# Output projections placed earlier among the sample streams, inverse roots on VectorE, expert loads issued in pieces, and a reordered rank chain

## The reference

```python
xn = rmsnorm(x, norm_mix_g)
q, k, v, f, B, C, h = split(xn @ w_in)            # 3*512 + 8 + 3*512 columns
o_a = forgetting_attention(q, k, v, f)            # 8 heads of 64; a stream also reads 128 cached rows
o_b = B * causal_conv3(C * h)                     # 512 channels
x = x + concat(rmsnorm(o_a, g_a), rmsnorm(o_b, g_b)) @ w_out
t = rmsnorm(x, norm_ffn_g)
g = top1(softmax(t @ w_rg + b_rg))                # 4 groups
e1, e2 = top2(softmax(t @ w_re[g] + b_re[g]))     # 8 experts in each group
x = x + sum(w_e * (silu(t @ gate_e) * (t @ up_e)) @ down_e for e in (e1, e2))
y = rmsnorm(x, norm_final_g)
```

## Time and profile before

| | |
|---|---|
| median of 3 runs | 546.57 us |
| the profiled execution's own time | 542.85 us |
| its span | 540.9 us |
| TensorE busy | 463.1 us (86%) |
| TensorE weight loads | 259.7 us (48%) |
| VectorE busy | 188.1 us (35%) |
| ScalarE busy | 125.2 us (23%) |
| mean granted clock of TensorE | 0.912 |
| bytes moved by DMA | 131.34 MB |

### The profile page before, as it was taken

How to read it: one execution, slowest core, us unless ns; L and a number is a source line. 1 busy time by engine, 2 the same in 40 slices (tenths; PEclk the granted TensorE clock), 3 DMA queues, 4 the chain that set the end, 5 groups by cost and what they waited for, 6 DMA issues and landing times.

```text
span 540.9 us, 6899 instructions
## 1 busy us (share of the span) xinstructions
PE 463.1 (86%) x2687; PEld 259.7 (48%) x2687; DVE 188.1 (35%) x555; ACT 125.2 (23%) x272; POOL 17.8 (3%) x49
## 2 busy tenths in 40 slices
PE   5999999999997979998569999799897998597580
PEld 4556545555656645644567357253533434152120
DVE  2200002424534425461644751244351425123234
ACT  4123213234224516554401110010010101010014
POOL 6000020000000000000000000001000000000000
PEclk9799999999996989998669996899898999889685
DMA  8997720000004942000805999999999999999702
GB/s 283 376 387 197 244 109 19 2 0 0 1 0 161 414 184 79 21 1 1 349 1 216 423 411 417 415 416 421 412 422 412 420 413 420 417 418 417 294 1 117
DMA packets 38232, 131.34 MB, mean 243 GB/s; under 512 B 10346, under 2 KB 10390, under 8 KB 30008
## 3 DMA queue, kind: packets, MB, share of 16 engines
q1 hardware_dynamic: 36928, 127.13, 60.0%
q10 hardware_dynamic: 664, 2.14, 1.0%
q0 software_dynamic: 608, 1.62, 0.8%
HBM read 127.68 MB, written 3.19 MB: 242 GB/s over the span
## 4 chain that ended last, share of the span: by engine, by line
PE 53%; DMA 31%; SPq 6%; DVE 4%; ACT 3%; issue 2%; DVEq 0%; ACTq 0%
PE bank L1465 50%; DMA gu_ring<-in_w_expert_gate_up 26%; SPq L533 3%; DMA r_xs<-in_cache_k 3%; DMA gu_ring<-in_w_in 2%; PE bank L1679 1%; PE bank L1585 1%; ACT L766 1%; DVE X L1453 1%; ACT r_xT L971 1%; SPq L545 1%; SPq L542 1%; PE bank L1649 0%; ACT r_xT L813 0%; DVE r_qz L1168 0%
## 5 line engine op out<-in xcount | busy, mean ns | idle before, releaser
L1465 PE MATMUL bank<-gu_ring,r_xT 128*32 128x512 f32 (+1 forms) x560 | 88.6, 670 | 23.5 <-DMA gu_ring<-in_w_expert_gate_up 23.5
L1465 PE MATMUL bank<-r_xT,gu_ring 128*128 128x384 f32 x192 | 66.4, 506 | 2.3 <-DMA gu_ring<-in_w_in 2.3
L1465 PEld LDWEIGHTS bank<-gu_ring,r_xT 128*32 128x32 f32 (+1 forms) x560 | 28.8, 128 | 80.3 <-issue 80.1
L1465 PEld LDWEIGHTS bank<-r_xT,gu_ring 128*128 128x128 f32 x192 | 37.6, 198 | 28.3 <-DMA gu_ring<-in_w_in 2.5
L1465 PE MATMUL bank<-BT,r_qz 128*128 128x128 f32 x384 | 46.4, 282 | 4.2 <-DVE BT L1271 4.2
L1465 PE MATMUL bank<-r_xs 128*128 128x512 f32 x96 | 49.8, 649 | 0.0
L1465 PEld LDWEIGHTS bank<-BT,r_qz 128*128 128x128 f32 x384 | 44.9, 197 | 10.2 <-issue 10.2
L1465 PE MATMUL bank<-r_xT,dn_ring 128*128 128x384 f32 x128 | 42.6, 486 | 0.0
L1345 DVE TENSOR_TENSOR X<-X,bank 128x512 f32<-128x512 f32 x48 | 33.0, 688 | 23.3 <-PE bank L1465 22.8
L1465 PE MATMUL bank<-dn_ring,V 128*32 128x512 f32 x256 | 31.3, 633 | 7.1 <-ACT V L917 4.3
L907 ACT ACTIVATE r_kT<-bank 128x256 f32<-128x256 f32 x8 | 3.1, 384 | 142.7 <-PE bank L1465 142.7
(11 more groups left out here) (293 smaller groups left out, 493.9 us busy)
## 6 DMA issues: line engine op xcount, KB each, us to landing
gu_ring<-in_w_expert_gate_up SPq DMA_DIRECT2D x64, 1024.0 KB, 18.8
dn_ring<-in_w_expert_down SPq DMA_DIRECT2D x32, 1024.0 KB, 20.3
gu_ring<-in_w_in SPq DMA_DIRECT2D x4, 2048.0 KB, 11.9
dn_ring<-in_w_in SPq DMA_DIRECT2D x2, 2048.0 KB, 19.1
gu_ring<-in_w_out SPq DMA_DIRECT2D x2, 2048.0 KB, 9.2
r_xs<-in_cache_k SPq DMA_DIRECT2D x8, 256.0 KB, 3.6
r_xs<-in_cache_v SPq DMA_DIRECT2D x8, 256.0 KB, 6.9
X<-in_x SPq DMA_DIRECT2D x3, 512.0 KB, 4.2
```

The source lines that it names most:

```text
L1465: return te.matmul(out, lhsT, rhs, start=start, stop=stop, **kw)
```

## The change

Output projections, sums and routing of tiles 0 and 1 have new steps; the twelve input projections leave out every fourth unit; the sums of tile 2 no longer go through the jobs. All inverse roots are made by VectorE: a first value from the bits of the number and three steps. x2's transposes read X itself, and the gain of the ffn norm goes into the router's weights (whose layout changes with it) and, with the root, into the gained rows. Quad 0's weights are issued in five places. The spare expert is chosen on VectorE from the counts, and loaded before quad 1. `gate_up(0)` stands before keys and slot weights; the overflow table and `swiglu(0)` before the picks of quad 1.

```diff
@@ jobs
         for f in range(3 * CT):
-            jobs_at.setdefault(1 + f, []).append(("ChB"[f % 3], f // 3))
-        first_oB = 3 * CT + 4
-        jobs_at[first_oB - 1] = [("ssB",)]
-        for i, keys in enumerate((
-                [("ssA", 0), ("oB", 0, 0)], [("oB", 0, 1)], [("oA", 0, 0)], [("oA", 0, 1)],
-                [("ssA", 1), ("oB", 1, 0)], [("oB", 1, 1)], [("x2", 0), ("oA", 1, 0)], [("lg", 0), ("oA", 1, 1)],
-                [("oB", 2, 0)], [("oB", 2, 1)], [("x2", 1)])):
-            jobs_at[first_oB + i] = keys
-        AFTER = [("lg", 1), ("ssA", 2), ("oA", 2, 0), ("oA", 2, 1), ("x2", 2), ("lg", 2)]
+            jobs_at.setdefault(1 + f + f // 3, []).append(("ChB"[f % 3], f // 3))
+        jobs_at.update({
+            2 * H: [("ssA", 0)], 2 * H + 1: [("oA", 0, 0)], 2 * H + 2: [("ssB",), ("oA", 0, 1)], 2 * H + 3: [("oB", 0, 0)],
+            2 * H + 4: [("ssA", 1), ("oB", 0, 1)], 2 * H + 5: [("oA", 1, 0)], 2 * H + 6: [("oA", 1, 1)],
+            2 * H + 7: [("oB", 1, 0), ("x2", 0)], 2 * H + 8: [("lg", 0), ("oB", 1, 1)], 2 * H + 9: [("oB", 2, 0)],
+            2 * H + 10: [("x2", 1), ("oB", 2, 1)], 2 * H + 11: [("lg", 1)]})
+        LAST_ROWS = 2 * H + 4
+        AFTER = [("oA", 2, 0), ("oA", 2, 1), ("x2", 2), ("lg", 2)]
@@ SyncE
+            sp.wait_ge(g_full, 2 * CT + TT)
+            for half in range(2):
+                load_up(0, 2, half)
+            sp.wait_ge(g_full, g_of["C", CT - 1] + 1)
+            load_down(0, 0)
+            load_down(0, 1)
+            sp.wait_ge(g_full, g_of["h", CT - 1] + 1)
+            load_down(0, 2)
+            load_down(0, 3)
             sp.wait_ge(s_full, 2 * H)
             for b in range(2, 4):
                 sp.dma_start(ck[b], a["cache_k"][b]).then_inc(ld_ck[b], 16)
             sp.wait_ge(g_full, g_of["B", CT - 1] + 1)
             for half in range(2):
-                for h in (2, 3):
-                    load_up(0, h, half)
-            for h in range(WIDE):
-                load_down(0, h)
-            sp.wait_ge(g_full, g_of["ssB",] + 1)
-            sp.dma_start(gbc, a["norm_ffn_g"].partition_broadcast(P)).then_inc(ld_gain, 16)
+                load_up(0, 3, half)
             for b in range(4, NB):
...
+                if b == 6:
+                    sp.wait_ge(g_full, g_of["ssB",] + 1)
+                    sp.wait_ge(last_done, CT)
+                    sp.dma_start(gbc, a["norm_ffn_g"].partition_broadcast(P)).then_inc(ld_gain, 16)
...
-            sp.wait_ge(g_full, g_of["oA", TT - 1, 1] + 1)
-            for half in range(2):
-                for h in (0, 1):
+            for h, key in ((1, ("oB", TT - 1, 1)), (0, ("oA", TT - 1, 1))):
+                sp.wait_ge(g_full, g_of[key] + 1)
+                for half in range(2):
                     load_up(0, h, half)
+            load_spare()
             for n in range(1, QUADS):
...
-                if n == 1:
-                    load_spare()
@@ ScalarE, after the loop
             square_a(TT - 1)
-            estimate(("ssA", TT - 1))
-            square(TT - 1)
+            act.wait_ge(st_out, 16 * 4)
+            square_last(0)
+            square_last(1)
             x2_evac(TT - 1)
-            estimate(("nr2", TT - 1))
-            scale_rows(TT - 1)
@@ VectorE
-            def inv_sqrt(out, n0, n1, done, count, ready=None):
-
-                dve.wait_ge(done, count)
-                link(v.tensor_tensor(nt[:, n0:n1], nr0[:, n0:n1], nr0[:, n0:n1], ALU.mult))
-                link(v.tensor_tensor(nt[:, n0:n1], nt[:, n0:n1], nv[:, n0:n1], ALU.mult))
-                link(v.tensor_scalar(nt[:, n0:n1], nt[:, n0:n1], -0.5, 1.5, ALU.mult, ALU.add))
-                ins = v.tensor_tensor(out, nt[:, n0:n1], nr0[:, n0:n1], ALU.mult)
+            def inv_sqrt(out, n0, n1, ready=None):
+
+                x, z, w = nv[:, n0:n1], nr0[:, n0:n1], nt[:, n0:n1]
+                link(v.tensor_single_scalar(z.bitcast(i32), x.bitcast(i32), 1, ALU.logical_shift_right))
+                link(v.tensor_scalar(z.bitcast(i32), z.bitcast(i32), -1.0, GUESS, ALU.mult, ALU.add))
+                for three in (-3.0, -12.0, -768.0):
+                    if n1 - n0 == 1:
+                        link(v.scalar_tensor_tensor(w, z, x, z, ALU.mult, ALU.mult))
+                    else:
+                        link(v.tensor_tensor(w, z, z, ALU.mult))
+                        link(v.tensor_tensor(w, w, x, ALU.mult))
+                    link(v.scalar_tensor_tensor(z, w, three, z, ALU.add, ALU.mult))
+                ins = v.tensor_single_scalar(out, z, -1.0 / 8192.0, ALU.mult)
...
-            job_evac(("lg", 1))
-            job_evac(("ssA", TT - 1))
-            rstd(("ssA", TT - 1))
+            dve.wait_ge(*g_place[g_of["lg", 1]])
+            route(1)
+            gained_rows(1)
+            dve.wait_ge(ssz_full, 1)
+            link(v.tensor_scalar(nv[:, TT - 1:TT], bS[0][:, 0:1], 1.0 / A, EPS, ALU.mult, ALU.add))
+            inv_sqrt(rs_ab[:, TT - 1:TT], TT - 1, TT)
             job_evac(("oA", TT - 1, 0))
             job_evac(("oA", TT - 1, 1))
+            rstd2_last()
             gained_rows(TT - 1)
-            nv2(TT - 1)
-            dve.wait_ge(*g_place[g_of["lg", 1]])
-            route(1)
-            rstd2(TT - 1)
             job_evac(("lg", TT - 1))
...
             dve.wait_ge(rk_full, 1)
-            dve.wait_ge(cnt_full, 1)
-            link(v.tensor_copy(rk[:, :, :], bT[0][:, 0:TT * E].rearrange("p (t e) -> p t e", t=TT)))
+            ranks = bT[0][:, 0:TT * E].rearrange("p (t e) -> p t e", t=TT)
             for c in range(2):
-                link(v.tensor_tensor(ohr[:, :, :], oh[:, c, :, :], rk[:, :, :], ALU.mult))
-                link(v.reduce_sum(pos[:, c, :], ohr[:, :, :], AX))
+                ins = v.tensor_tensor(ohr[:, c, :, :], oh[:, c, :, :], ranks, ALU.mult)
+            link(ins)
+            link(v.reduce_sum(pos[:, :, :], ohr[:, :, :, :], AX))
...
+            pick_step(0)
+
+            dve.wait_ge(cnt_full, 1)
+            link(v.tensor_copy(cnt[:, :], bS[1][:, 0:E]))
+            link(v.tensor_scalar(e0[:, :], cnt[:, :], float(SLOTS), float(E), ALU.is_le, ALU.mult))
+            link(v.tensor_tensor(e0[:, :], e0[:, :], iota_e[:, :], ALU.add))
+            link(v.tensor_reduce(e0_key[:, 0:1], e0[:, :], AX, ALU.min))
+            v.tensor_scalar(spare_reg[:, 0:1], e0_key[0:1, 0:1], float(E - 1), None, ALU.min).then_inc(spare_set, 1)
...
+            ins.then_inc(rw_done, 1)
+            overflow_table()
+            swiglu(0)
+            dve.wait_ge(keys_full, 1)
+            pick_step(1)
...
-            v.tensor_scalar(nv[:, 0:TT], ss[:, 0:TT], 1.0 / D, EPS, ALU.mult, ALU.add).then_inc(nv3_done, 1)
+            link(v.tensor_scalar(nv[:, 0:TT], ss[:, 0:TT], 1.0 / D, EPS, ALU.mult, ALU.add))
+            inv_sqrt(rs3[:, :], 0, TT)
             for t in range(TT):
-                v.tensor_tensor(X[:, t, :], X[:, t, :], gbc, ALU.mult).then_inc(y3_done, 1)
-            dve.wait_ge(y3_done, TT)
-            inv_sqrt(rs3[:, :], 0, TT, nr3_done, 1)
-            for t in range(TT):
-                v.tensor_scalar(yo[t], X[:, t, :], rs3[:, t:t + 1], None, ALU.mult).then_inc(out_done, 1)
+                v.scalar_tensor_tensor(yo[t], X[:, t, :], rs3[:, t:t + 1], gbc, ALU.mult, ALU.mult).then_inc(out_done, 1)
@@ TensorE
-            for key in AFTER:
-                job(key)
+            job(("oA", TT - 1, 0))
+            last_squares()
+            job(("oA", TT - 1, 1))
+            job(("x2", TT - 1))
+            job(("lg", TT - 1))
...
             pick_rows(0)
+            gate_up(0)
...
             ins.then_inc(w_full, 1)
-            gate_up(0)
```

259 lines of the change are left out of this document (126 added, 133 removed).

## The result

The changed kernel takes **515.51 us** (median of 4 runs, 513.24 to 516.53), the kernel before beside it 546.26 us (4 runs, 541.98 to 547.23): a ratio of 0.9431, 95% interval 0.9401 to 0.946. Beside the first experiments it ran four times more, median 516.82; over all eight runs the median is 516.14, and the experiments are set against that. The profiled execution took 515.05 us, span 513.0.

The account below looks back on a forecast made before the run. TensorE bounds the first half; after M, when half of quad 0's gate and up product ends and releases quad 1's loads, the expert-weight queue does. Terms sum to 25.0 us off 542.85: 517.9, by the median 521.5 us; range 514 to 531.

Parts of the forecast that it names:

- F: After quad 1's loads are released: spare expert loaded earlier saves 7.6 us, about 3.6 lost to idle DMA; 4.0 us gain.
- A: Input projections spread over units 1 to 15: unit 15 ends 9.5 us earlier, ssB takes 3.15 back; 6.4 us gain.
- B: Streams: earlier weight loads and no ScalarE root estimates remove waits of 2.88 and 1.76 us; 6.0 us gain.
- C: Last projection to tile 2's one-hots: transposes of X, split square and VectorE roots bring 3.1 us.
- D: Ranks to first picks: ranks no longer wait for the counts, and the chain loses operations; 2.0 us gain.
- G: The end, after the last add to X: VectorE root operations and three two-tensor passes; 1.0 us gain.
- E: Quad 0's gate and up right after its picked rows, ahead of keys and slot weights: quad 1's loads released 2.5 us sooner.
- Rival 1: TensorE bounds quads 0 to 2: clock drops behind the wait before quad 1's picks, losing all 7.6 us and more; 527.5 us, chance 0.17.
- Rival 2: VectorE becomes the bound of the streams, B is nothing and A 5; 529 us, chance 0.12.
- Rival 3: Slower than before: low clock stays through 58 us of TensorE work until mid quad 2's product; 560 us, chance 0.02.
- Rival 4: Queue not freed: spare's number reaches SP late, 7.6 us stay in the saturated stretch; 525.5 us, chance 0.07.
- Rival 5: Clock is kept through ranks and picking too, 4 us more gain; 517 us, chance 0.1.

Follow-up runs that it names:

- jobs_1to12: Changed kernel with the twelve input projections back in units 1 to 12: 518.9 us, ratio 0.9504.
- keys_between: Changed kernel with the keys' matmuls between the two halves of quad 0's gate and up product: 515.14 us, ratio 0.945.
- gate_after_keys: Changed kernel with quad 0's gate and up product back behind keys and slot weights, quad 1's picks ahead of its swiglu: 516.64 us, ratio 0.9446.
- combined: Changed kernel with keys between product halves, squares spread, tile 2's gained rows split, and filling matmuls early and in the last quad: 508.14 us, ratio 0.9296.
- roots_end: Changed kernel with the three inverse roots behind the loop back on ScalarE's Ln and Exp: 520.79 us, ratio 0.9517.
- again: The changed kernel itself, unedited, run a second time: 516.82 us, ratio 0.9446.
- loads_together: Changed kernel with quad 0's early weights (8 MB) all issued behind the last input projection: 525.28 us, ratio 0.959.
- roots_streams: Changed kernel with the five inverse roots amid the streams back on ScalarE's Ln and Exp: 515.99 us, ratio 0.9454.
- ssb_amid: Changed kernel with the 24 one-column matmuls of the convolution rows' squares spread between the same unit's projection matmuls: 514.83 us, ratio 0.9414.
- early_fill: Changed kernel with tile 2's gained rows split and filling matmuls ahead of the ranks and first picks: 513.05 us, ratio 0.9385.
- spare_late: Changed kernel with the spare expert's six loads back behind quad 1's: 520.75 us, ratio 0.956.
- tail_fill: Changed kernel with 8 and 7 filling matmuls during TensorE's waits in the last quad: 515.98 us, ratio 0.9448.

## Why the prediction was right, and where not

**The number.** 521.5 was forecast and 515.5 measured, inside 514 to 531, faster as by 0.96. Of the 6 us, 2.9 are terms of the sum (27.9 of span instead of 25.0). Another 2.9 are the medians: the profiled run of before stood 3.4 us below its median, that of after 0.5, so the medians lie further apart than the spans. The rest is the median of before, now 0.3 lower. The prediction allowed for this scatter but took the offset over to both kernels. Of the 2.9 us of terms 2.6 stand under F, and are luck of the profiled run, as shown there.

**A, 6.4.** The wait at unit 14 went and unit 15 ended at 165.96 (165.2 forecast). The step that was mis-sized is "ssB, now in unit 18, takes 3.15 back": it took 2.84, and 1.7 more by the slow projection behind it (5.38 against 3.70). In profiles that kept the clock that second part is nothing. By the jobs experiment, 3.5 of the 8.8 us by which unit 15 ends earlier are the spread itself; the rest is ssB, taken from its place behind the wait.

**B, 6.0.** With A it makes 12.9 against 12.4, so B is about 8.6 when A is 4.3. The 2.88 us wait went by the earlier loads, and their experiment shows this is the heart of it. The step that failed is the second: "without the estimates by ScalarE it goes". The run that gives them back to ScalarE hasn't got the wait. It was two roots together, 5.94 us, that held the evacuation up; with the new order they stand in different units. That is read from the traces, no edit tests it. The 1.2 us that I took off for longer VectorE work and the turned outputs were too much: waits amid the streams sum to under 1.1 us, and 0.64 ahead of the next to last projection. Without them B would have been 7.2, so 1.4 of the 8.6 us are in no term.

**C and D** held to 0.1 us, and term by term: in C the half square took 0.73, the linked operations 2.1 and the gained rows 2.13. The experiment gives 1.7 of C's 3.1 to the root without table loads; the rest, and D, have no experiment of their own.

**G** came to 0.9 for 1.0, but not by its sum, and that is luck. Its rows add up to 0.6 (535.9 in place of 536.5); the rest was put to the outputs that spread more. In the traces VectorE's last pass ends 11.0 us behind the last add before and 11.2 after (at 509.68), since the three passes take 3.68 and not 3.4 and the sums of squares come 0.4 later. The gain lies behind it: 3.3 us from there to the span's end in place of 4.4. The wider spacing of the outputs fits that; it wasn't tested.

**E, 2.5**, was 2.3 to M and is worth nothing at the end, since F pays for it. The prediction had both halves in its sum, so the sum was right; a reader of the single terms would be misled.

**F, 4.0**, was 6.6 in the first profile: 5.2 by L less M, and 1.4 from L to the last add by a better clock. Most of the 2.6 us above the forecast is luck: with 232.5 to 232.8 us from M to the last add in the four other profiles with picks of 7.25 us, F is 3.9 to 4.1. The mechanism was right as far as it went: quad 3's loads, released by the first half of quad 2's product, were issued at M + 64.0 (M + 64.4 forecast), where the queue had run dry. It overlooked that the queue runs short twice before: in the changed kernel 328 GB/s in 290 to 295 us and 356 in 300 to 305, besides 254 in 330 to 335, where keys_between has 407, 421 and 421. Over all kernels with the spare's loads early, L less M goes by how long quad 1's picks take:

| quad 1's picks | profiles | L less M |
|---|---|---|
| 5.62 us, no wait | gate_after_keys, keys_between, combined | 205.9, 205.9, 206.1 |
| 5.62 us, wait of 2.4 | jobs_1to12, roots_end | 205.9, 205.7 |
| 7.25 us, wait of 2.4 | after, again, loads_together, roots_streams, ssb_amid | 208.3, 209.0, 209.1, 209.4, 208.7 |
| 8.52 us, wait of 2.4 | early_fill | 210.0 |

213.5 less 205.9 is 7.6, the price of the spare's bytes. So the full term is there when the clock is kept, and the wait by itself costs nothing that shows: in jobs_1to12 the down weights of quad 1 are still issued at M + 18.9, before the 20 us of transfer ahead of them (8.4 MB) are over, and quad 2's first loads at M + 28.9; after a slow picking these are M + 20.6 and M + 30.5. So it is the 1.6 us of clock behind the wait that make the issues come too late, and 2.4 to 3.5 us are lost with it (4.1 after the slowest picks). The 3.6 that I took off had nearly this size, but the step behind it was wrong: "That is 5.3 us later, and 1.4 us more", the first by the order of the work and the second by the clock, was carried in full to quad 3's loads. Quad 1's picks did start 5.3 us later (M + 8.6 in place of M + 3.3). But against M + 57.7 before, the release of quad 3's loads comes 3.1 us later by the order (M + 60.8 in jobs_1to12), which costs nothing at L, and 3.2 more behind slow picks (M + 64.0). This is read from kernels that differ by chance in their clock; no edit sets the clock alone.

**Rivals.** Rival 1 had the mechanism, a clock that drops behind the new wait and picks of 7.25 us, in 8 of the 10 profiles that have the wait (spare_late and tail_fill, whose L can't be compared, among them), but its price was 2.4 to 4.1 us and not all of the 7.6 and 2 more. The Trainium skill, TensorE: Matmul & The Clock Gate, section "HAM oscillation", describes a TensorE that waits between short bursts of matmuls and starts each at the low rate. The direction agrees, but this isn't its case: here TensorE had been busy for 17 us (257.61 to 274.69) before the wait of 2.39, and two profiles with the same wait kept the full clock. Rival 2 is out: VectorE releases no wait above 0.57 us amid the streams. Rival 3 is out, no slice stays low. Rival 4 is out by the trace, where the spare's six issues stand at 259.38 to 262.92, 5.5 us ahead of M, and by spare_late. Rival 5 did not come: the first picks took 7.23 us. In early_fill they took 5.60, 1.6 less; the rival had put 4 us on the whole stretch.

**The criterion.** "The last load lands more than 215 us after M" came true by its letter, though the forecast held. The last of all loads, the down weights, landed 218.6 us after M (TensorE waits for them until 487.03). The 215 was the bytes of seven quads over 416.5 GB/s, 211.4 us, and some margin, and that was too tight for any outcome: in gate_after_keys, where the queue doesn't run dry, TensorE still waits for the last down weights until 216.2 us after M. The last gate and up weights, by which I should have put it, came at 208.3.

## What to carry to other kernels

When a load queue sets the pace behind a serial stretch, count two things for each piece of work that you move. The first is when the queue is released. The second is how far each later release stands from the moment at which the queue runs dry. A gain at the first release can be paid for at the later ones: here E's 2.3 us were, and the keys placed between the two halves of a product kept the gain at M (24.8 us behind the last projection) and also the 205.9 us from M to L. Roots of one column are best done where no activation table has to be loaded for them, but only where the root is on the path. And one profile of each kernel isn't enough to size a term: F read 6.6 us in the first and 3.9 in the second. Move loads with the work that they feed: with quad 0's weights issued in one place as before, the last projection came 9.4 us later (loads_together).
